# First two modulation vectors in four column slices beside the first two units; later vectors requested by ScalarE

## The reference

```python
mod = (silu(c) @ w_ada + b_ada).reshape(B, 9, 1024)      # nine vectors: shift, scale, gate, three times
h = modulate(x, s1, sc1)                                 # x * (1 + scale) + shift
x = layer_norm(ALPHA * x + 0.5 * (1 + g1) * swiglu(h, ffn1_wgu, ffn1_wdown))
h = modulate(x, s2, sc2)
u_pool, u_lru, u_gate = split(h @ w_in)                  # 512 columns each
y_pool = windowed means of u_pool, times w_pool, scaled
y_lru = gelu(u_gate) * rglru(causal_conv(u_lru))         # a scan over the rows
x = layer_norm(ALPHA * x + (1 + g2) * (concat(y_pool, y_lru) @ w_out))
h = modulate(x, s3, sc3)
x = layer_norm(ALPHA * x + 0.5 * (1 + g3) * swiglu(h, ffn2_wgu, ffn2_wdown))
```

## Time and profile before

| | us |
|---|---|
| median of 3 runs | 1069.49 (1068.58 to 1071.79) |
| the profiled execution | 1070.84 |
| its span | 1068.8 |
| TensorE busy | 1002.8 |
| VectorE busy | 618.4 |
| ScalarE busy | 456.1 |
| moved by DMA | 234.75 MB, 220 GB/s over the span |

### The profile page before, as it was taken

One profiled execution on the slowest core, in us unless ns is written; L12 is line 12 of the kernel. 1 busy time (PEld: TensorE's weight loads), 2 busy tenths in 40 slices (PEclk: granted clock), 3 DMA queues, 4 the chain that ended last, 5 costly groups with the idle time before them and its releaser, 6 DMA issues.

```text
span 1068.8 us, 21885 instructions
## 1 busy us (share of the span) xinstructions
PE 1002.8 (94%) x9648; PEld 971.5 (91%) x9648; DVE 618.4 (58%) x919; ACT 456.1 (43%) x564; POOL 110.5 (10%) x171
## 2 busy tenths in 40 slices
PE   4798999999994999999999999999998989999996
PEld 3698999998994899999999999999997979999995
DVE  1535545457894664544467555445689856555464
ACT  1434334334482444433345444432548444444342
POOL 4030000000610140000004200000050023000000
PEclk9899999999998999999999999999998989999998
DMA  9898976984739268885974998877753627765521
GB/s 301 265 323 236 317 229 229 314 292 150 276 106 308 80 184 269 237 282 191 317 196 152 265 303 227 301 276 253 261 196 130 188 80 201 195 170 168 177 100 41
DMA packets 279234, 234.75 MB, mean 220 GB/s; under 512 B 7328, under 2 KB 240922, under 8 KB 279123
## 3 DMA queue, kind: packets, MB, share of 16 engines
q1 hardware_dynamic: 277040, 229.70, 68.8%
q0 software_dynamic: 1792, 2.54, 0.9%
q10 hardware_dynamic: 306, 1.12, 0.3%
HBM read 232.06 MB, written 1.78 MB: 219 GB/s over the span
## 4 chain that ended last, share of the span: by engine, by line
PE 58%; DVE 7%; DMA 2%; issue 1%; ACT 1%; SPq 1%; DVEq 0%; ACTq 0%
PE bank L456 18%; PE bank L457 17%; PE bank L458 17%; PE bank L481 3%; DMA raw<-in_ffn_wgu_dram 2%; PE bank L467 2%; ACT w_hi L744 1%; DVE w_lo L954 1%; DVE rstd L1044 1%; DVE xc L1217 1%; SPq L328 0%; DVE z L1034 0%; PE bank L619 0%; DVE z L1022 0%; SPq L304 0%
## 5 line engine op out<-in xcount | busy, mean ns | idle before, releaser
L456 PE MATMUL bank<-m_hi,w_hi 128*128 128x264 f32 x1664 | 479.5, 288 | 21.6 <-DVE m_lo L1065 10.7
L954 DVE TENSOR_TENSOR w_lo<-raw,w_hi 128x2048 fp32r<-128x2048 f32 (+2 forms) x156 | 337.8, 2166 | 245.9 <-ACT w_hi L744 245.4
L457 PE MATMUL bank<-m_lo,w_hi 128*128 128x264 f32 x1664 | 474.8, 285 | 0.0
L458 PE MATMUL bank<-m_hi,w_lo 128*128 128x264 f32 x1664 | 474.0, 285 | 0.0
L744 ACT ACTIVATE w_hi<-raw 128x2048 fp32r<-128x2048 f32 (+2 forms) x156 | 280.0, 1797 | 204.8 <-PE bank L458 164.6
L456 PEld LDWEIGHTS bank<-m_hi,w_hi 128*128 128x128 f32 x1664 | 316.3, 190 | 27.3 <-issue 18.0
L457 PEld LDWEIGHTS bank<-m_lo,w_hi 128*128 128x128 f32 x1664 | 316.6, 190 | 0.1
L458 PEld LDWEIGHTS bank<-m_hi,w_lo 128*128 128x128 f32 x1664 | 315.2, 189 | 0.0
L456 PE MATMUL bank<-h_hi,w_hi 128*128 128x264 f32 x672 | 193.9, 288 | 0.0
L458 PE MATMUL bank<-h_hi,w_lo 128*128 128x264 f32 x672 | 191.0, 284 | 0.0
L457 PE MATMUL bank<-h_lo,w_hi 128*128 128x264 f32 x672 | 190.8, 284 | 0.0
(11 more groups left out here) (204 smaller groups left out, 522.1 us busy)
## 6 DMA issues: line engine op xcount, KB each, us to landing
raw<-in_ffn_wgu_dram SPq DMA_DIRECT2D x168, 512.0 KB, 5.3
ada_raw<-in_w_ada_dram SPq DMA_DIRECT2D x72, 1024.0 KB, 9.8
raw<-in_ffn_wdown_dram SPq DMA_DIRECT2D x48, 512.0 KB, 3.5
raw<-in_ffn_wdown_dram SPq DMA_DIRECT2D x48, 384.0 KB, 4.3
raw<-in_w_in_dram SPq DMA_DIRECT2D x24, 512.0 KB, 4.7
raw<-in_w_out_dram SPq DMA_DIRECT2D x16, 384.0 KB, 7.3
raw<-in_w_out_dram SPq DMA_DIRECT2D x8, 256.0 KB, 6.8
x_rows<-in_x_prompt_dram ACTq DMA_DIRECT2D x1, 1024.0 KB
```

What stands on the lines that cost most here:

```text
L456: pe.matmul(out, hi, r_hi, start=start, stop=False)
L457: pe.matmul(out, hi, r_lo, start=False, stop=False)
L458: mm = pe.matmul(out, lo, r_hi, start=False, stop=stop)
L954: dve.tensor_tensor(w_lo[:, g % SLOTS, 0:n], raw[:, g % SLOTS, 0:n], w_hi[:, g % SLOTS, 0:n].bitcast(F32), ALU.subtract).then_inc(lo_split, 1)
```

## The change

The four chunk buffers now take, for vectors 0 and 1, slices of 256 columns with all 1024 rows (1 MB, in runs of 1 KB), shift and scale in turn: eight slices, in which the first two units are embedded (slices 0, 1, unit 0, slices 2, 3, unit 1, slices 4 to 7). TensorE sums each slice in four row groups, ScalarE copies it (`slice_copy`, into the one `part`), and a matmul with `sum_w` adds the groups and turns them. VectorE forms two tiles of the input from each pair (`slice_input`, `slice_low`), ScalarE their high parts (`slice_high`). From the second pair on TensorE runs the products of units 0 and 1 together, two tiles behind each pair. The bias of layer 0 is turned by itself ahead of that; the other parameters and states of layer 0 are turned behind unit 5, those of layer 1 behind unit 7, and GpSimd requests them after unit 1's low part, the head weights after unit 5's. Half of the copies of `x` go to ScalarE. Vectors 2 to 17 are requested by ScalarE: vector 2 after the split of unit 2, each later half right behind the `ada_copy` of the same half of its predecessor. Three vectors move by one or two units.

```diff
-    AFTER = {2: (7, 1), 3: (14, 1), 4: (20, 1), 5: (26, 1), 6: (32, 0), 7: (38, 0), 8: (52, 1), 9: (60, 1),
+    AFTER = {2: (9, 1), 3: (15, 1), 4: (20, 1), 5: (26, 1), 6: (32, 0), 7: (38, 0), 8: (53, 1), 9: (60, 1),
              10: (68, 1), 11: (77, 0), 12: (85, 1), 13: (92, 1), 14: (98, 1), 15: (104, 1), 16: (110, 0),
              17: (122, 0)}
     FIRST_HALF = {AFTER[a][0]: a for a in AFTER if AFTER[a][1]}
 
-    ADA_BANK = {a: (6, 7, 6, 6) for a in range(VECTORS)}
-    ADA_BANK[0], ADA_BANK[1] = (6, 7, 3, 3), (6, 7, 6, 5)
-    ADA_BANK[17] = (0, 1, 6, 6)
-
-    LOAD_BEHIND = {2: (4, 5)}
-    for a in range(3, VECTORS):
-        first, apart = AFTER[a - 1]
-        LOAD_BEHIND[a] = (first + 6, first + 6 + apart)
-    BEHIND = {}
-    for a, units in LOAD_BEHIND.items():
-        for h, u in enumerate(units):
-            BEHIND.setdefault(u, []).append((a, h))
...
-            def load_ada(a, chunks):
-                for c in chunks:
-                    if a:
-                        sync.wait_ge(ada_used, (a - 1) * CHUNKS + c + 1)
-                    sync.dma_start(ada_raw[:, c], ada_view[a // NMOD, a % NMOD, c // 2, c % 2])\
-                        .then_inc(ada_landed[c], 16)
-
-            load_ada(0, range(CHUNKS))
-            load_unit(0)
-            load_ada(1, range(CHUNKS))
-            for g in range(1, ALL_UNITS):
+            def load_slice(i):
+
+                c, first = i % ADA_SLOTS, i % 2 * D + i // 2 * SLICE
+                if i >= ADA_SLOTS:
+                    sync.wait_ge(ada_used, i - ADA_SLOTS + 1)
+                sync.dma_start(ada_raw[:, c].rearrange("p k d -> p (k d)").rearrange("p (k d) -> p k d", d=SLICE),
+                               w_ada[0].rearrange("(k p) d -> p k d", p=P)[:, :, first:first + SLICE])\
+                    .then_inc(ada_landed[c], 16)
+
+            for i in range(2 * SLICES):
+                load_slice(i)
+                if i in (1, 3):
+                    load_unit(i // 2)
+            for g in range(2, ALL_UNITS):
                 load_unit(g)
-                for a, h in BEHIND.get(g, ()):
-                    load_ada(a, (2 * h, 2 * h + 1))
...
+            load_bias(0)
+
+            ready(pool, 1)
             load_rows(0)
+            load_bias(1)
+            load_rows(1)
+            ready(pool, 5)
             load_heads(0)
-
-            ready(pool, 3)
-            load_rows(1)
...
-            pe.wait_ge(init_read, 1 + DT)
+            pe.wait_ge(bias_landed, N_BIAS * 16)
+            transpose_rows(bank[5][:, 0:120], p_rows[0][0:120, :]).then_inc(bias_out, 1)
...
+            def slices(q):
+
+                for i in (2 * q, 2 * q + 1):
+                    b, src = bank[6 + i % 2], ada_raw[:, i % ADA_SLOTS].rearrange("p k d -> p (k d)")
+                    pe.wait_ge(ada_landed[i % ADA_SLOTS], (i // ADA_SLOTS + 1) * 16)
+                    if i >= 2:
+                        pe.wait_ge(slice_read, i - 1)
+                    for k in range(DT):
+                        g = k % 4
+                        mm = pe.matmul(b[32 * g:32 * g + 32, 0:SLICE], cT[:, k, :],
+                                       src[:, k * SLICE:(k + 1) * SLICE], start=k < 4, stop=k >= 4,
+                                       tile_position=(0, 32 * g))
+                    mm.then_inc(ada_used, 1)
+                for i in (2 * q, 2 * q + 1):
+                    pe.wait_ge(slice_part, i + 1)
+                    for j in range(2):
+                        mm = pe.matmul(bank[6 + i % 2][:, SLICE + 32 * j:SLICE + 32 * j + 32], part[:, j],
+                                       sum_w[:], start=True, stop=True)
+                    mm.then_inc(slice_out, 1)
+
+            def first_units():
+                slices(0)
+                pe.wait_ge(init_read, 1 + DT // 2)
+                pe.wait_ge(init_read_act, DT // 2)
+                ready(pe, 0)
+                for q in range(1, SLICES):
+                    slices(q)
+                    if q == 1:
+                        ready(pe, 1)
+                    products(0, 0, 2 * q - 2)
+                    products(0, 0, 2 * q - 1)
+                products(0, 0, DT - 2)
+                products(0, 0, DT - 1)
...
-                    if l == 0 and f == 0 and n == 11:
-                        pe.wait_ge(param_landed[1], N_ROWS * 16)
-                        pe.wait_ge(mod_read, 3)
-                        prepare(1, bank[6], bank[7])
+                    if l == 0 and f == 0 and n in (5, 7):
+                        pe.wait_ge(param_landed[n // 7], N_ROWS * 16)
+                        if n == 5:
+                            pe.wait_ge(slice_read, 2 * SLICES)
+                        else:
+                            pe.wait_ge(prep_read, 2)
+                            pe.wait_ge(bias_landed, DEPTH * N_BIAS * 16)
+                        prepare(n // 7, bank[6], bank[7])
...
+            def request(n, chunks):
+                for c in chunks:
+                    act.dma_start(ada_raw[:, c], ada_view[n // NMOD, n % NMOD, c // 2, c % 2])\
+                       .then_inc(ada_landed[c], 16)
+
             def ada_copy(a, h):
                 act.wait_ge(ada_used, a * CHUNKS + 2 * h + 2)
                 act.activation(part[:, h], bank[ADA_BANK[a][h]][:, 0:P], ACT.Copy).then_inc(part_ready, 1)
+                if a < VECTORS - 1:
+                    request(a + 1, (2 * h, 2 * h + 1))
...
+            def slice_copy(i):
+                act.wait_ge(ada_used, i + 1)
+                if i:
+                    act.wait_ge(slice_out, i)
+                act.activation(part[:].rearrange("p h d -> p (h d)"), bank[6 + i % 2][:, 0:SLICE], ACT.Copy)\
+                   .then_inc(slice_part, 1)
+
+            def slice_high(q):
+                act.wait_ge(sample_full, q + 1)
+                for m in (2 * q, 2 * q + 1):
                     act.activation(m_hi[:, m], sq[:, m], ACT.Copy).then_inc(m_hi_done, 1)
...
-            ada_copies(0)
+            for m in range(1, DT, 2):
+                act.wait_ge(init_out, 2 + m)
+                act.activation(x[:, m], bank[1 + m % 4][:, 0:T], ACT.Copy).then_inc(init_read_act, 1)
+            slice_copy(0)
+            slice_copy(1)
             split(0)
-            ada_copy(1, 0)
-            first_input(0, 0, 4)
-            ada_copy(1, 1)
-            first_input(1, 4, 4)
+            slice_high(0)
+            slice_copy(2)
+            slice_copy(3)
             split(1)
+            slice_high(1)
+            for q in range(2, SLICES):
+                slice_copy(2 * q)
+                slice_copy(2 * q + 1)
+                slice_high(q)
             split(2)
+            request(2, range(CHUNKS))
...
+            def slice_input(q):
+
+                t = slice(2 * q, 2 * q + 2)
+                for i, v in ((2 * q, S1), (2 * q + 1, SC1)):
+                    turned = bank[6 + i % 2][:, SLICE:SLICE + 64].rearrange("p (m c) -> p m c", c=32)[:, :, 0:C]
+                    dve.wait_ge(slice_out, i + 1)
+                    dve.tensor_tensor(coef[:, 1 - v, t], turned,
+                                      bias_mod(0)[:, v, t].unsqueeze(2).broadcast_to([P, 2, C]), ALU.add)\
+                       .then_inc(slice_read, 1)
+                dve.wait_ge(slice_read, 2 * q + 2)
+                dve.wait_ge(init_read_act, DT // 2)
+                for m in (2 * q, 2 * q + 1):
+                    own.did(dve.tensor_scalar(sq[:, m, 0:TP], x[:, m, 0:TP], coef[:, 0, m, 0:1], coef[:, 1, m, 0:1],
+                                              ALU.mult, ALU.add))
...
+            dve.wait_ge(bias_out, 1)
+            take_bias(0, bank[5][:, 0:120])
+            own.wait()
+            slice_input(0)
             split(0)
-            take_parameters(0, bank[0], bank[1])
-            own.wait()
-            finish_vector(0)
-            dve.wait_ge(half_out, 1)
-            own.did(dve.tensor_tensor(mod[:, SC1, 0:4], half_turned(1, 0), bias(1, 0, 4), ALU.add))
-            dve.wait_ge(mod_read, 1)
-            first_coefficients(0, 4)
-            first_samples(0, 0, 4)
-            take_states(0, bank[0], bank[1])
-            first_lows(0, 4)
-            finish_vector(1)
-            dve.wait_ge(mod_read, 2)
-            first_coefficients(4, 4)
-            first_samples(1, 4, 4)
-            first_lows(4, 4)
+            slice_low(0)
+            slice_input(1)
             split(1)
+            slice_low(1)
+            for q in range(2, SLICES):
+                slice_input(q)
+                slice_low(q)
```

More of the change, by code:

```diff
@@ L518, in prepare, with products @@
                     transpose_rows(b1[:, m * 32:(m + 1) * 32], r_rows[l][:, m * P:(m + 1) * P])
-                transpose_rows(b1[:, 128:248], p_rows[l][0:120, :])
+                if l:
+                    transpose_rows(b1[:, 128:248], p_rows[l][0:120, :])
                 transpose_rows(b1[:, 248:284], q_rows[l][0:36, :]).then_inc(prep_out, 1)
-            def up_phase(l, f, together, vector):
+            def products(l, f, k):
```

(37 more changed lines are left out.)

144 lines of the change are left out of this document (61 added, 83 removed).

## The result

The changed kernel takes 1071.35 us (median of 20 runs, 1068.92 to 1073.41) against 1069.30 (20 runs, 1067.43 to 1071.79): a ratio of 1.0020, 95% interval 1.0013 to 1.0027. It is 2 us slower, within 0.3%, where 1057.0 was predicted. The profiled execution has a span of 1070.2 us against 1068.8.

What follows compares the result with a forecast made beforehand. TensorE, busy 94% of 1068.8 us, bounds the kernel where fed. Start 1.5, layer 0's output projection 10.8 and around 600 us 0.5 sum to 12.8: profiled 1070.84 becomes 1058.0, stated as 1057 for the median, range 1047 to 1066.

Steps and rivals of the forecast that it cites:

- The requests on ScalarE: Vector requests moved to ScalarE, 0.5 us an issue: 10.8 us gained in layer 0's output projection, between 8 and 12.5.
- Unit 45's wait: Layer 0's output projection: VectorE's 10.99 us wait goes, split done by 332.3, residuals end 9.0 us sooner.
- The 1.8 us in it for the clock: End of layer 0's output projection: TensorE idles some 4 us instead of 14, clock stays up, 1.8 us gained.
- The signs: Unit 2 at 54 to 61 us, no long unit 6 wait, prompt unit 45 split, clock up near 340, requests 0.4 to 0.9.
- The rule: Shared DMA engines: a second issuer saves only issue time, so vector 8 would still delay unit 45 and the 10.8 us be lost.
- that rival: Third rival, layer 0's output projection: vector bytes still go ahead of unit 45's, the wait stays, 1068.8 us; chance 5%.
- Rival 1: ScalarE held at each request for 3.567 us, at the start and in the output projection: slower, 1082 us; chance 7%.
- The start: First units embedded in a new slice order: unit 2 at 58.4 us, 1.5 us gained in all, between -5 and +6.
- The 4.7 us of unit 6: Start, ahead of unit 6: the 3.45 us wait and 1.3 us of low clock go.
- Rival 2: Start stays at the lower clock, all 96 products of units 0 and 1 at 0.2 us: 1062.5 us; chance 15%.
- Around 600 us: Vector 12 requested before unit 83, not between it and 84: the 0.54 us lost there go, counted as 0.5.
- rival 4: Start goes well, clock up from the first products and input 1.5 us sooner: about 4 less, 1053 us; chance 18%.

Runs made afterwards that it cites:

- e1: Changed kernel with vectors 7 and 17 requested behind ScalarE's split of the mixer's last input unit (38 and 116): 1062.31 us.
- e5: Changed kernel with vectors 7 and 17 requested late and vector 8 requested in the next up phase (units 47 and 48): 1056.24 us.
- e3: Kernel before the change with one edit, SyncE requesting vector 8 behind units 47 and 48 instead of unit 44: 1054.68 us.
- e4: Changed kernel with 8 extra identity matmuls on TensorE ahead of each of the waits for units 0 and 1: 1063.35 us.
- e12: Changed kernel with later vectors requested by SyncE as before the change, vector 8 behind units 47 and 48, 8 and 8 extra start matmuls: 1049.17 us.
- e2: Changed kernel's new start alone, vectors 2 to 17 requested by SyncE at the places of the kernel before: 1070.32 us, ratio 1.0009.
- after: The changed kernel itself, with the whole change and no further edit: 1071.35 us, ratio 1.0020 against the kernel before.
- e6: Changed kernel with 8 and 8 extra matmuls ahead of the waits for units 0 and 1, and nine ahead of the wait for x: 1061.74 us.
- e10: Changed kernel with requests for vectors 7 and 17 each split into two of half the columns, giving 1 KB packets: 1065.08 us.
- e8: Changed kernel with only the second halves of vectors 7 and 17 requested late, behind the splits of units 38 and 116: 1061.46 us (one run).

## Why the prediction was wrong, step by step

- **The requests on ScalarE** is the step that failed. It priced the 64 issues and the load of unit 45, and put the vectors' bytes ahead of every other load at nothing, without a reason. Vector 7 moved from behind unit 38 to 3.2 us ahead of it: 3.5 us of layer 0's mixer (e1). Vector 8, which the forecast had nearly landed by 320 us, was asked for from 311 us on, and its packets run from 312 to 329, beside those of units 43 and 44, and unit 45's start only at 329: 8.5 us (e5). With both, 2.5 of the 10.8 us were left. My answer to the rule against the change, that vector 8 comes "into a stretch where few loads run", was wrong.
- **Unit 45's wait** itself went as forecast (0.31 us), and its price was sound: 12.3 us alone (e3) against 10.8. But the split was forecast for 330 us and starts at 337.60, since VectorE comes late to it. The 1.8 us in it for the clock did not come either: TensorE stands 3.28 us ahead of the statistics (some 4 were forecast), and the mean runs as slowly as before (2.85 us; 1.51 in e4, e5 and e12).
- **Layer 1** was left out of the sum. Vector 17 repeats vector 7's move with nothing to win in return: 4.6 us, all of it back in e1.
- **The signs.** Most of the signs that were to show the forecast right were met: unit 2 at 60.88, no wait ahead of unit 6, the split of unit 45 at once, a median of 0.525 us a request. They looked at the places that were to gain, and none at a load that could lose.
- **The rule.** The Trainium skill, page DMA: Bandwidth & Descriptors, section Issuing engines are not separate DMA queues, has it that all issuers share 16 engines. The trace agrees (both queues at once, 375 GB/s from 276 to 282 us). By that rule I reckoned 1068.8 with the wait still ahead of unit 45; the wait went, another came, and 1068.8 was nearer than 1057. The chance of 5% for that rival was too small, since it covered only one place.
- **Issue cost.** 0.5 us each was right: the 64 requests take 0.374 us at least, 0.525 in the median, 1.843 at most. Rival 1 (3.567 each) did not come.
- **The start.** Unit 2 was forecast at 58.4 and began at 60.88 in this execution, 58.48 to 60.88 over six. Mis-sized were the low-clock terms: the sums of one slice 1.06 us and not 0.36, a pair of slices 3.64 and not 2.8 to 3.0, the first products 5.6 and not 5.0. The 2.8 was the mean of a stretch that ran at both speeds (the kernel before has 44 records in its first 2.2 us and 64 in the next 2.0), so it was no price of the low clock. The 4.7 us of unit 6 did go, and `prepare(0)` costs TensorE 1.05 us (84.33 to 85.38) and not 1.37; its twin turns one block more. The input was there 0.7 us sooner (11.96 against 12.65), as forecast. Rival 2 (all 96 products at the lower clock) did not come; the clock rose with the second round. As a whole the start is even (e2), not 1.5 better.
- **Around 600 us** 0.8 instead of 0.5: right (with SyncE's requests e2 and e12 have 210.6 and 210.5 there, the others 210.1 to 210.3).

The range, 1047 to 1066, missed too: each bound varied the size of the gains, none an order of loads that I had not looked at. Its lower end also counts the clock of the start twice, in rival 4 and in the +6, and rivals 1 and 3 are set against the profiled execution, 2 and 4 against the median; neither decides here.

## What to carry to other kernels

When requests move to another queue, list for each the loads that follow within its transfer time, and ask which of them has a date; here a queue of its own added no bandwidth (375 GB/s with both, 386 with one), it took away the order. Moving one request to a place where nobody waits (one line, e3) was worth more than the whole change. And where TensorE waited in short steps at the start, eight idle matmuls in each of two waits were worth 3.6 to 6 us.

## What the runs showed of the hardware that I had not expected

- **Queues take turns by packets.** Two queues with work sent nearly equal numbers of packets, whatever their size: 743 of 2 KB to 745 of 1 KB (after), 1173 of 2 KB to 1145 of 512 B (e6), 1084 to 1004 of 1 KB each (e10). Bytes go by packet size: 1.49 to 0.75 MB, 2.32 to 0.58, 1.07 to 1.00. The Trainium skill, page DMA: Bandwidth & Descriptors, section Queues, rings and completion order, says that an engine drains one whole packet, typically 9 to 17 descriptors, from a ring and goes on to the next. The counts agree with taking turns; the packets counted here are single runs of 512 B to 2 KB, and whether the packets of the Trainium skill hold as many runs on both queues no row shows. I had not used it.
- **A load starts late on busy engines.** Unit 38's first packet starts 4.0 us after its request in after (271.48 to 275.45), 3.9 in e8 and 4.2 in e10, and 1.3 us after it in e1 (269.30 to 270.61) and in the kernel before, where no vector ran. In the first three it starts at about the time at which the vector's first 2 MB have been sent. Why is open.
- **The clock record.** From 36 to 40 us the windows give a granted clock (third figure from the end of a row) of 1.00 in after and of 0.50 in e1, whose program is the same there, while the products go at 0.22 us in both:

```profile
36.00:40.00 4.00, 1.39 (x6) 1.40 (x7) 3.21 (x6) 0.74 (x2) 1.16 (x3) 1.00 1.12 331
```

```profile
36.00:40.00 4.00, 3.18 (x14) 3.18 (x15) 1.45 (x3) 0.00 (x0) 2.94 (x6) 0.50 1.15 318
```

The first row is after's, the second e1's (their products began at 38.61 and 36.82). At 264 columns in 0.22 us a product the engine was at the lower of its two levels (1.2 GHz) in both, so a 1.00 in this column is to be set against the spacing of the matmuls. In e4 the column reads 1.00 too; there the spacing of 0.12 us agrees.
